# RWKV bonus bank read one step earlier, and identity products in front of four kinds of TensorE waits

## The reference

```python
def rwkv7_time_mix(rw, z, mu, w_up, w0, a_up, a0, k_k, k_a, r_k, gn_gain, gn_bias):
    ...
    kk = l2norm(heads(k * k_k.astype(f32)))
    k = k * (1.0 + (a - 1.0) * k_a.astype(f32))
    r_h, k_h, v_h = heads(r), heads(k), heads(v)
    o = rwkv7_scan(r_h, heads(decay), k_h, v_h, kk, heads(a))
    o = layernorm(o, gn_gain.reshape(N_HEADS, HEAD_DIM), gn_bias.reshape(N_HEADS, HEAD_DIM), RWKV_GN_EPS)
    o = o + jnp.sum(r_h * k_h * r_k.astype(f32), axis=-1, keepdims=True) * v_h
    return (o.reshape(B, T, MIX_WIDTH) * jax.nn.silu(z.astype(f32))).astype(z.dtype)
```

## Time and profile before

| what | us |
|---|---|
| median of 3 runs | 4019.72 |
| lowest and highest run | 4011.29, 4024.91 |
| the profiled execution's own time | 4012.28 |
| its span in the profile | 4010.5 |
| PE busy | 3772.6 (94% of the span) |
| DVE busy | 2630.1 (66%) |
| mean granted TensorE clock | 0.965 of full |

### The profile page before, as it was taken

The page is one execution under the profiler, slowest core; times in us unless marked ns, Lnnn a source line. Parts: engine busy times, 40 slices in busy tenths (PEclk is TensorE's granted clock), DMA queues, the critical chain, the costliest instruction groups (busy, mean ns, idle before and its releaser), DMA issues.

```text
span 4010.5 us, 51700 instructions
## 1 busy us (share of the span) xinstructions
PE 3772.6 (94%) x20718; PEld 2957.9 (74%) x20718; DVE 2630.1 (66%) x2926; ACT 1343.8 (34%) x1756; POOL 1193.1 (30%) x578
## 2 busy tenths in 40 slices
PE   8999899999889999999999998999999989998998
PEld 7567788877666666778887776887777767776777
DVE  6964887789874554378788988741455454547783
ACT  5243432234333333243223434211333232324522
POOL 2012144444313333214444441222222212222064
PEclk9999999999989999999999998999999989999999
DMA  3002233345320010222324532323312222323063
GB/s 114 21 21 89 100 101 107 108 154 183 120 80 32 32 37 22 90 105 89 108 93 166 181 121 96 109 91 107 125 59 69 82 72 72 118 89 95 34 209 142
DMA packets 131768, 385.57 MB, mean 96 GB/s; under 512 B 13564, under 2 KB 14208, under 8 KB 126280
## 3 DMA queue, kind: packets, MB, share of 16 engines
q1 hardware_dynamic: 131528, 382.27, 27.5%
HBM read 281.00 MB, written 101.22 MB: 95 GB/s over the span
## 4 chain that ended last, share of the span: by engine, by line
PE 71%; DVE 22%; ACT 4%; issue 1%; POOL 1%; DMA 1%; DVEq 0%; SPq 0%; ACTq 0%; POOLq 0%
PE ps L380 22%; PE ps L1453 21%; PE ps L476 9%; PE ps L4476 2%; PE ps L907 2%; PE ps L2250 1%; PE ps L2971 1%; DVE top L1626 1%; DVE acc L1722 1%; PE ps L2242 1%; DVE xop L1626 1%; PE ps L3064 1%; DVE x L661 1%; PE ps L2988 1%; DVE t L641 1%
## 5 line engine op out<-in xcount | busy, mean ns | idle before, releaser
L333 POOL TENSOR_TENSOR wlo<-wraw,whi 128x1024 fp32r<-128x1024 f32 x181 | 447.8, 2474 | 1712.1 <-ACT whi L325 1703.7
L1453 PE MATMUL ps<-xop,whi 128*128 128x512 f32 x1984 | 617.7, 393 | 14.7 <-DVE acc L1747 9.8
L325 ACT ACTIVATE whi<-wraw 128x1024 fp32r<-128x1024 f32 x185 | 196.1, 1060 | 887.6 <-PE ps L380 605.4
L1453 PE MATMUL ps<-top,whi 128*128 128x512 f32 x1488 | 470.7, 398 | 19.7 <-DVE acc L1716 15.9
L1453 PEld LDWEIGHTS ps<-xop,whi 128*128 128x128 f32 x1984 | 373.0, 188 | 99.7 <-DVE acc L1747 12.3
L1453 PE MATMUL ps<-xop,wlo 128*128 128x512 f32 x992 | 388.2, 391 | 0.0
L476 PE MATMUL ps<-xhalf,whi 128*128 128x512 f32 x1024 | 369.7, 443 | 0.2 <-POOL wlo L333 0.2
L1453 PEld LDWEIGHTS ps<-top,whi 128*128 128x128 f32 x1488 | 282.3, 190 | 88.3 <-DVE acc L1716 19.1
L1851 POOL TENSOR_TENSOR wlo<-wsum,whi 128x1024 fp32r<-128x1024 f32 (+2 forms) x102 | 228.9, 2244 | 363.5 <-ACT whi L1478 363.0
L380 PE MATMUL ps<-xhi,whi 128*128 128x512 f32 x868 | 306.7, 435 | 18.8 <-DVE xlo L681 6.7
L1453 PE MATMUL ps<-top,wlo 128*128 128x512 f32 x744 | 294.7, 396 | 0.0
(11 more groups left out here) (641 smaller groups left out, 7091.4 us busy)
## 6 DMA issues: line engine op xcount, KB each, us to landing
wraw<-in_w_dram SPq DMA_DIRECT2D x185, 512.0 KB, 3.6
h_keep<-h SPq DMA_DIRECT2D x154, 256.0 KB, 4.5
wraw<-in_s_dram SPq DMA_DIRECT2D x48, 512.0 KB, 4.1
f<-h_keep SPq DMA_DIRECT2D x24, 768.0 KB, 5.4
wmore<-in_s_dram SPq DMA_DIRECT2D x32, 512.0 KB, 4.0
x_keep<-x SPq DMA_DIRECT2D x16, 1024.0 KB, 3.8
g_keep<-gates SPq DMA_DIRECT2D x64, 256.0 KB, 2.4
gb<-g_keep SPq DMA_DIRECT2D x32, 512.0 KB, 4.1
```

Source lines behind the costliest of these rows:

```text
L325: se.own().activation(K.hi(c), K.raw[:, c % NRAW, :], ACT.Copy).then_inc(*K.S(("hi", c)))
L333: ge.own().tensor_tensor(K.lo(c), K.raw[:, c % NRAW, :], K.hi(c).bitcast(F32), SUB).then_inc(*K.G(("lo", c)))
L1453: d = pe.e.matmul(out[:, s, :], w[:, o], x[:, i, :], start=(j < 3 and i == 0 and t == 0), stop=(i == k - 1 and t == 2), skip_group_check=True)
```

## The change

`keep_busy` issues a number of products of the 128x128 identity with itself, in float32, into the bank that has just been taken; nobody reads them, and the real product then overwrites the bank. They stand behind the wait for the bank and ahead of the wait for the operands: 10 in the first unit of GDN, ahead of its first spread; and in each of the four RWKV units 4 ahead of the sums of kk, 5 ahead of the bonus's spread, and 3 ahead of the first pairs. That is 58 in all. On DVE the read of the bonus's bank moves ahead of the scaling of RO, from the next step into this one. As it now comes ahead of the `norm` that still reads the former unit's bonus, BON becomes two tiles, one for each q.

```diff
+def keep_busy(pe, K, b, products):
+
+    for _ in range(products):
+        pe.e.matmul(K.ps[:, b, 0:128], K.ident, K.ident, start=True, stop=True, skip_group_check=True)
+
+
+def sums_tensor(pe, K, Q, H, n, *squares, busy=0):
 
     b = take(pe, K, Q, n, "sum")
+    keep_busy(pe, K, b, busy)
     pe.wait_ge(*K.at(n, "sq"))
...
+def spread_tensor(pe, K, Q, n, ones, src, *ready, halves=1, busy=0):
...
         b = take(pe, K, Q, n, h)
+        keep_busy(pe, K, b, busy)
         for ev in ready:
             pe.wait_ge(*K.at(*ev))
...
+def pairs_tensor(pe, K, Q, n, p, lhs, rhs, *ready, busy=0):
 
     b = take(pe, K, Q, n, "pairs")
+    keep_busy(pe, K, b, busy)
...
+        spread_tensor(pe, K, Q, (n, "gb"), H.pair[0:4, j, :], H.rows[0:4, HALVES[q]], ("small rows",), busy=0 if before else 10)
...
+            self.R0, self.O, self.WT, *self.BON = (sb(s0, 512)[:, :] for _ in range(5))
...
+        sums_tensor(pe, K, Q, H, (n, "kk"), B.pad, busy=4)
...
+        spread_tensor(pe, K, Q, (n, "bonus"), H.heads, B.Aa, (n, "bonus in"), busy=5)
         yield
+        pairs_tensor(pe, K, Q, ((n, 0), "a"), part(0, 64), B.BE, B.AL, (n, "al"), (n, "be"), busy=3)
...
         ve.own().tensor_tensor(KA, KA, Cs, MUL).then_inc(*V((n, "ka")))
+        ve.wait_ge(*K.at((n, "bonus"), "mm", 0))
+        ve.own().tensor_tensor(B.BON[q], K.bank((n, "bonus"), 0), Vv, MUL).then_inc(*V(("free", ((n, "bonus"), 0))))
         ve.own().tensor_tensor(RO, RO, B.pad, MUL).then_inc(*V((n, "ro")))
         yield
-        ve.wait_ge(*K.at((n, "bonus"), "mm", 0))
-        ve.own().tensor_tensor(B.BON, K.bank((n, "bonus"), 0), Vv, MUL).then_inc(*V(("free", ((n, "bonus"), 0))))
```

More of the change, by code:

```diff
@@ L2865, in put_away @@
     e.e.dma_start(K.keep_y[i], src).then_inc(*W.out(event, ("y kept", i)))
-def sums_tensor(pe, K, Q, H, n, *squares):
+def keep_busy(pe, K, b, products):
+    for _ in range(products):
+        pe.e.matmul(K.ps[:, b, 0:128], K.ident, K.ident, start=True, stop=True, skip_group_check=True)
+def sums_tensor(pe, K, Q, H, n, *squares, busy=0):
     b = take(pe, K, Q, n, "sum")
+    keep_busy(pe, K, b, busy)
     pe.wait_ge(*K.at(n, "sq"))
@@ L2932, in turn_scalar @@
         se.own().activation(dst[:, 4 * q:4 * q + 4, :], v4(K.bank(n, q)), ACT.Copy).then_inc(*K.S((n, "rows"), ("free", (n, q))))
-def spread_tensor(pe, K, Q, n, ones, src, *ready, halves=1):
+def spread_tensor(pe, K, Q, n, ones, src, *ready, halves=1, busy=0):
     for h in range(halves):
         b = take(pe, K, Q, n, h)
+        keep_busy(pe, K, b, busy)
         for ev in ready:
@@ L3055 @@
 INVERSE_STEPS = 13
-def pairs_tensor(pe, K, Q, n, p, lhs, rhs, *ready):
+def pairs_tensor(pe, K, Q, n, p, lhs, rhs, *ready, busy=0):
     b = take(pe, K, Q, n, "pairs")
+    keep_busy(pe, K, b, busy)
     for ev in ready:
@@ L3110, in first @@
         n = ("gdn", j, q)
-        spread_tensor(pe, K, Q, (n, "gb"), H.pair[0:4, j, :], H.rows[0:4, HALVES[q]], ("small rows",))
+        spread_tensor(pe, K, Q, (n, "gb"), H.pair[0:4, j, :], H.rows[0:4, HALVES[q]], ("small rows",), busy=0 if before else 10)
         spread_tensor(pe, K, Q, (n, "bb"), H.pair[32:36, j, :], H.rows[32:36, HALVES[q]])
@@ L3505, in __init__ @@
         with Scope(way.side) as s0:
-            self.R0, self.BON, self.O, self.WT = (sb(s0, 512)[:, :] for _ in range(4))
+            self.R0, self.O, self.WT, *self.BON = (sb(s0, 512)[:, :] for _ in range(5))
             self.Vt, self.A0, self.K1, self.B1 = (sb(s0, 4, 128) for _ in range(4))
@@ L3534, in first @@
         yield
-        sums_tensor(pe, K, Q, H, (n, "kk"), B.pad)
+        sums_tensor(pe, K, Q, H, (n, "kk"), B.pad, busy=4)
         yield
@@ L3541, in first @@
         yield from wait_steps(2)
-        spread_tensor(pe, K, Q, (n, "bonus"), H.heads, B.Aa, (n, "bonus in"))
+        spread_tensor(pe, K, Q, (n, "bonus"), H.heads, B.Aa, (n, "bonus in"), busy=5)
         yield
-        pairs_tensor(pe, K, Q, ((n, 0), "a"), part(0, 64), B.BE, B.AL, (n, "al"), (n, "be"))
+        pairs_tensor(pe, K, Q, ((n, 0), "a"), part(0, 64), B.BE, B.AL, (n, "al"), (n, "be"), busy=3)
         pairs_tensor(pe, K, Q, ((n, 0), "b"), part(0, 64), B.KA, B.AL, (n, "ka"))
@@ L3741, in norm @@
         ve.own().tensor_scalar(B.O, B.O, K.vec("rw_gn_gain", j), K.vec("rw_gn_bias", j), MUL, ADD).then_inc(*V())
-        ve.own().tensor_tensor(B.O, B.O, B.BON, ADD).then_inc(*V())
+        ve.own().tensor_tensor(B.O, B.O, B.BON[q], ADD).then_inc(*V())
         z = W.ZY[:, HALVES[q]]
```

## The result

| | median, us | runs, us | ratio to before, 95% interval |
|---|---|---|---|
| before, beside it | 4015.03 | 4007.93 to 4025.98 | |
| changed | 4024.01 | 4019.47 to 4034.19 | 1.0021 [1.0014, 1.0029] |
| changed, in a later session | 4023.40 | 4014.20 to 4029.77 | 1.0014 [1.0001, 1.0026] |

The changed kernel is slower by 6 to 9 us. The forecast was 0.4 us faster. The time lies inside the range and within the 0.3% that was called no change, but the sign is the other one, and it holds in both sessions. The profiled execution of the changed kernel took 4031.29 us (span 4029.5), high among its runs, as that of before, 4012.28, was low among its own. A part of the 19 us between the two traces is thus only the executions; the experiments say which part.

What follows compares the result with a forecast made beforehand. The prediction took PE, busy 803.9 of 850 us in the scans and partly at half clock, as the main bound. Terms +7.2 - 1.9 + 0.8 - 1.7 - 4.0 gave 0.4 us faster: 4019 us from 4019.72, range 4003 to 4029.

Steps and rivals of the forecast that it cites:

- What bounds the kernel: Whole kernel: mostly PE, partly at half clock; an identity product costs its length except where PE waits longer than it lasts.
- The move, +7.2: Earlier read of the bonus's bank on DVE: 2.4 us gained per unit in three RWKV units, 7.2 us faster.
- The new wait, -1.7: Ahead of the fourth pairs product: PE waits 2 to 3 us, one half-clock fall over three units, 1.7 us slower.
- Rival (B): Fourth pairs product: stall moves there and grows, clock falls 6.8 us in every unit; 13.3 us slower, 4033; chance 0.07.
- Four ahead of the sums, -1.9 + 0.8: Sums of kk: products paid in units two and three, 1.9 us slower; clock kept in the first, 0.8 us faster.
- Eight ahead of bonus and pairs, 0: Five products ahead of the bonus, three ahead of the first pairs, per RWKV unit: hidden in waits, cost 0.
- Ten at the start, -4.0: First GDN spread, behind the wait for all engines: ten products paid at half clock, 4.0 us slower (0.5 to 5.0).
- The sum: Whole kernel: +7.2 - 1.9 + 0.8 - 1.7 - 4.0 = +0.4 us faster, 4019 on the median.

Runs made afterwards that it cites:

- e13: Kernel before plus the move of the bonus's read and the products ahead of the bonus (five) and first pairs (three) in each unit: 4016.61 us, ratio 0.9999.
- e1: Kernel before plus only the move of the read of the bonus's bank, no identity products: 4018.19 us, ratio 1.0006.
- e6: Kernel before plus 16 identity products ahead of the wait for all engines at the start of the scans: 4016.85 us, ratio 0.9999.
- e14: Kernel before plus the move and four more gate steps in the new wait of units two and three, no identity products: 4021.31 us, ratio 1.0010.
- e2: Kernel before plus only the ten identity products at the start of the scans: 4019.42 us, ratio 1.0010.
- e5: Kernel before plus only 30 identity products at the start of the scans, where the change has ten: 4023.64 us, ratio 1.0016.
- e8: Kernel before plus the move and 12 identity products ahead of the fourth pairs product in units two to four: 4015.87 us, ratio 1.0005.
- e11: Kernel before with only 14 gate steps taken out of clumps in the scans, to run in the last stage: 4022.16 us, ratio 1.0017.
- e12: Kernel before plus the move and only the four identity products ahead of the sums of kk in each unit: 4021.75 us, ratio 1.0014.
- e3: Changed kernel without the ten products at the start; the move and the 48 RWKV products stay: 4020.80 us, ratio 1.0017 to the kernel before.
- e4: Kernel before plus the 48 identity products in RWKV, without the move and the ten at the start: 4014.72 us, ratio 0.9996.

## Why the prediction was wrong

**What bounds the kernel** was read rightly: an identity product was paid where PE did not wait (the ten, the sums), and free where it did (e13).

**The move, +7.2.** This is the step that failed. Its first half is right to a tenth: 3676 and the pairs come when I said, 3271 has no wait, and the first mask is 1.8 us early in units two to four. From there I took 2.4 us for gained "in a unit", without following the unit to its end. PE's path through the fourth product, the transposes and the gates is the longer one by then, and only 0.0 to 0.5 us are left of 1.8 at the second copy of bv. In e1 it is -0.1, 1.0 and 0.9 us of 1.8, and the kernel measured 1.0006 [0.9994, 1.0018], at most 2.4 us faster: the +7.2, or +5.5 with the next term, is not there.

**The new wait, -1.7.** Right in place, wrong in size and in what follows. I gave it 2 to 3 us and one fall of the clock in three; it is 3.5 to 4.6 us with a fall each time. The slip is arithmetic that I could have done: PE reached the fourth product in the kernel before at 3101.96 after doing its steps at half clock, so without the stall ahead of them, at full clock, it would be there some 7 us sooner. In the changed kernel it is there at 3110.84, 9.7 us behind the bonus input at 3101.10; before it was 16.8 (3101.96 less 3085.14). DVE's first mask is only 1.8 us sooner, and the rest becomes PE's new idle time. Rival (B) said just this: the stall moves to DVE's chain, and decides itself where the wait goes over 3 us. I gave it 0.07. Its mechanism came, though not its 4033 us: the stretches at these places are 6.8 us each, where before they were 10.2, 6.8 and 6.8. My argument against it was that the first unit has this wait and no fall follows. That was one trace's luck. Nine traces have 2.8 to 3.0 us of wait at that place; in four (before, e1, e6, e14) no half clock is near it, in five (e2, e5, e8, e11, e12) there is.

**Four ahead of the sums, -1.9 + 0.8.** The direct price was right: 0.88 and 0.89 us in units two and three (from the spread ahead of them to the sums 10.88 and 9.51 us before, 11.76 and 10.40 after). The +0.8 for the first unit came in some executions: the four left 1.23 of its 2.12 us of wait, and the half clock behind it is gone in e3, e4 and e12, where the bonus input comes 1.5 us earlier behind the sums (23.0 against 24.5 us). In both traces of the changed kernel it is there as before; all eleven traces without the four have it. The rest of e12's loss, in its trace the 13.6 us stretch in the second unit, is in no term of mine, and its cause stays open.

**Eight ahead of bonus and pairs, 0.** Right (e13, e4), for the reason given.

**Ten at the start, -4.0.** Right in size as far as the interval tells: 4.54 us of products, 3.8 at the first gate evacuation, 1.0010 [0.9998, 1.0023] in e2. The argument for it was wrong in one point: the products do release the clock (e5); the ten end too soon to have anything of it. And I had missed the load that hides the half clock there (e6).

**The sum.** Without the terms that failed: -1.9 - 4.0 = -5.9 us, where 1.0021 and 1.0014 are 8.4 and 5.6. By the parts: ten 4.0 (e2), move 2.4 (e1), four ahead of the sums 3.2 (e12 less e1), the eight -2.8 (e13 less e1), together 6.8 us slower, each with some 5 us of interval. Only the sum is clear of the noise, not the parts. The forecast's plus is missing because the move's 1.8 us never left the unit; that the kernel is slower, and not equal, comes from terms of which two were forecast (the ten, the sums' direct price).

## What to carry to other kernels

A shortened stall is worth what arrives at the end of the stage, not at the next instruction: follow both engines from the moved step to the point where the stage's serial chain begins, and compute when each would reach the next place where they meet. Where one engine gains 7 us and the other 1.8, the rest is a new wait, and with it comes the half clock.

Products that hold the clock belong ahead of a wait, in front of its semaphore, and only as many as fit in it; behind the wait they are paid in full. Before paying for full clock at a place, look what else ends there: a load or another engine may hide the slow stretch.

Where the clock falls and rises differs between executions of the same instructions, here by 6 us in a stretch of 30. One trace each of before and after can't carry a difference of a few us; segments between fixed instructions, over several traces, can. Even then look through all traces for the effect: a stretch in four traces of four seemed to be made by four products, until e11 and e1 showed its like without them.

## What the runs showed of the hardware

In the sixteen traces a product of the pairs line waited 3.3 us or more 27 times. In 25 of these the clock fell to half before the wait ended, or was there already, in one as it ended, and in one 1.5 us later. With 2.84 us of 128x128 identity products in such a wait and 2.08 us idle behind them it stayed at full (e8, mean clock 1.00 over the 12 us). Shorter waits went either way for the same instructions: 2.8 to 3.0 us in the first unit had half clock near them in five traces of nine. The wait of 2.12 us ahead of the first unit's sums had 3.4 us or more of half clock behind it in all eleven traces that keep it; where four identity products left 1.23 us of it, in two of five.

Thirty identity products behind a wait of 3.86 us brought full clock back 5.6 us after the first of them (e5); behind the same wait, ten products, the spread and gates took 9.4 us in one trace and 12.3 and 12.4 in two others until it rose.

Half clock also came where PE had not waited: 13.6 us of it with PE busy in all of them (e11 and e1, above), some 60 to 70 us into a unit. In the second unit four traces of four with the same two edits had it, none of three with the move and without the other, but also e14 and e11; in the third unit e1, e3 and e12. Which instruction brings it, if one does, is not shown.
